# Value products moved behind the next round's scores, and the probabilities divided by ScalarE, in a two-layer trunk kernel

## The chip, the cores and the metric

The kernel runs on one core of a Trainium2 chip. A core has five engines that run in parallel and meet only at semaphores: TensorE (PE, matrix products, with its weight loads shown apart as PEld), VectorE (DVE), ScalarE (ACT), GpSimd (POOL) and SyncE (SP), which here issues the transfers. Each engine takes its own instructions strictly in the order in which the program lists them, so an instruction that waits holds everything behind it on its engine. The metric is the device time of one execution in microseconds (us). The kernel before takes 1017.55 us, the median of 3 runs (1016.76 to 1018.16).

## The reference

Two layers of a decoder trunk on 256 positions of width 1024, in fp32. What matters here is the attention of a layer: 16 heads (A) with a learned sink, and 12 heads (C) in three dilation groups, whose outputs are weighted by their softmax denominators.

```python
for l in range(DEPTH):                                  # DEPTH = 2
    z = rms_norm(x, norm1_g[l]) @ w_in[l] + b_in[l]     # 1024 -> 8448: A, B, C and three gates
    # A and C: banded attention, head size 64
    s = q @ k.T * hd ** -0.5, masked
    m = max(s, -1)                                      # A: also the head's sink
    p = exp(s - m)
    denom = sum(p, -1)                                  # A: + exp(sink - m)
    o = (p / denom) @ v
    # B: spatial gating unit
    x = x + (sum_i sigmoid(gate_i) * (branch_i @ P_i)) @ w_out[l]
    x = x + hier_moe(rms_norm(x, norm2_g[l]), ...)      # 32 experts, top 2 of one group
out = rms_norm(x, norm_f_g)
```

## The kernel before

A layer is a trunk stage (projection, attention, gating, output projection) and an expert stage. The trunk multiplies by weights that stream in through a ring of slots. Every weight slot is a "conv" j: ScalarE rounds it to a high part (`high`, L954), VectorE takes the rest as a low part (`low`, L1161), and PE runs three passes (hi x hi, hi x lo, lo x hi, lines L1509 to L1511) for two halves of the slot and two blocks of 128 positions. A conv is 12 matmuls. Four convs fill one pair of PSUM banks with 512 columns of z, which VectorE then moves out (`z_out`, L1180); for the convs from 44 on this is banks 6 and 7, which every fourth conv starts afresh.

Attention is threaded between the convs 44 to 67, in rounds b = 0 to 11. Rounds 0 to 7 carry two A heads each, rounds 8 to 11 three C heads. In this text the pieces of PE's work have short names:

- Q(b): transposes of q and k for batch b (`qk`, L1613). ScalarE moves them out of PSUM to `qkt` (`qk_out`, L1030). Batches 8 and 10 need three such banks: the first and, for 8, the third go out by ScalarE, the second by VectorE (`swap_out`, L1340 and L1341). Batch 10's third is VectorE's too (L1347). Only two PSUM banks (3 and 4) serve all transposes in turn, so a transpose waits until the one two before it has been moved out (`bank_for`, `turn_taken`, semaphores t_evac and t_swapped). The third transpose of batch 8, called Q3(8) here, stands between the two halves of conv 58.
- S(b): the scores (L1632). VectorE scales, masks and takes the row maximum (`softmax_in`, L1275, L1285), ScalarE takes the exponentials and their row sums (`exps`, L1037), VectorE forms one over the denominator (`softmax_out`, L1303 and L1304, or L1306 to L1309) and multiplies the probabilities with it (L1312).
- T(b): transposes of the divided probabilities (`turn_probs`, L1644), which wait for p_ready. ScalarE moves them out (`pv_out`, L1051).
- P(b): the value products (`product_pair`, L1660, for b below 8; `products`, L1677, for 8 and 9 together after round 9, and for 10 and 11 at the end). ScalarE moves their result out (`o_out`, L1056).

Round b on PE before the change is: conv 44+2b, S(b+1), T(b), conv 45+2b, P(b), Q(b+2), where Q(9) and Q(11) don't exist. ScalarE's list in a round: high 46+2b, pv_out(b), exps(b+1), o_out(b), qk_out(b+2), high 47+2b. VectorE's: softmax_in(b+1), low 46+2b, in odd rounds z_out, in round 6 and 8 swap_out(b+2), softmax_out(b+1), low 47+2b. No scheduler is at work: the order on each engine is the order in which the code calls these helpers.

Of the kernel before, what the change touches and what calls it, by code (L numbers as in the profile page):

```python
# [15 lines left out]
ALU = mybir.AluOpType  # L16
# [8 lines left out]
P = 128  # L25
# [53 lines left out]
def trunk_program(nc, x, positions, norm1_g, w_in, b_in, attn_sinks, sgu_ln_g, sgu_ln_b, w_spatial,  # L79
# [7 lines left out]
    with ExitStack() as whole:  # L87
# [228 lines left out]
        neg_ready = sem("neg_ready")  # L316
# [347 lines left out]
        def trunk_stage(l):  # L664
            with ExitStack():
# [75 lines left out]
                with ExitStack():  # L741
# [191 lines left out]
                    def _(act):  # L933
# [98 lines left out]
                        def exps(b):  # L1032
                            act.wait_ge(neg_ready, 2 * b + 1)
                            i = b % 2
                            for n in range(heads(b)):
                                for tb, lo, hi in ((0, 0, P), (1, P, 3 * P)):
                                    act.activation(probs[:, i, n, lo:hi], probs[:, i, n, lo:hi], ACT.Exp,  # L1037
                                                   bias=neg[:, i, tb, n:n + 1], accum_out=den[:, i, tb, n:n + 1])
                            act.wait_ge(neg_ready, 2 * b + 2)
                            act.activation(ex[:, i, :, 0:heads(b)], ex[:, i, :, 0:heads(b)],  # L1040
                                           ACT.Exp).then_inc(exp_ready, 1)

# [35 lines left out]
                        high_at(45)  # L1078
                        qk_out(1)
                        for b in range(BATCHES):  # L1080
                            if b == 7:
                                halves_at(60)
                            else:
                                high_at(46 + 2 * b)
                            if b == BATCHES - 1:
                                high_at(47 + 2 * b)
                            pv_out(b)
                            if b == 8:
                                qk_out(b + 2, 0, 1)
                            if b == BATCHES - 2:  # L1090
                                high_at(47 + 2 * b)
                            if b + 1 < BATCHES:
                                exps(b + 1)
                            if b < BATCHES - 1:
                                o_out(b)
                            if b + 2 < BATCHES:
                                qk_out(b + 2, 1 if b == 8 else 0)
                            if b < BATCHES - 2:
                                high_at(47 + 2 * b)
                            if b in SPLITS:  # L1100
                                o_high(SPLITS.index(b))
# [37 lines left out]
                    def _(dve):  # L1139
# [125 lines left out]
                        def softmax_in(b, between=None):  # L1265
# [19 lines left out]
                            dve.tensor_scalar(neg[:, i, :, 0:n], m, -1.0, None, ALU.mult).then_inc(neg_ready, 1)  # L1285
                            if b < 8:
                                dve.tensor_tensor(ex[:, i, :, 0:n], sk, m, ALU.subtract).then_inc(neg_ready, 1)

                        def group_max(b):
# [5 lines left out]
                                              ALU.subtract).then_inc(neg_ready, 1)  # L1295

                        def softmax_out(b):
# [4 lines left out]
                            if b < 8:  # L1302
                                link(dve.tensor_tensor(d, d, e, ALU.add))  # L1303
                                link(dve.reciprocal(d, d))  # L1304
                            else:
# [3 lines left out]
                                link(dve.tensor_tensor(d, e, bcast(mxg[:, i, :].unsqueeze(2), [P, TB, n]), ALU.mult))  # L1309
# [169 lines left out]
                    def _(pe):  # L1479
# [202 lines left out]
                        def pv(b, between=None):  # L1682
# [6 lines left out]
                            gates_conv(45 + 2 * b, (lambda: turn_probs(b, 2)) if b >= 8 else None)  # L1689
                            if b < 8:  # L1690
                                product_pair(b)
                            elif b % 2:
                                products(b)
# [16 lines left out]
                        for b in range(BATCHES - 1):  # L1710
# [5 lines left out]
                            else:  # L1716
                                scores(b + 1)
                                pv(b)
# [938 lines left out]
```

## Time and profile before

| what | us |
|---|---|
| median of 3 runs | 1017.55 |
| the profiled execution, its own time | 1017.79 |
| its span on the core | 1015.8 |
| PE busy in the span | 956.4 (94%) |
| DVE busy | 561.1 (55%) |
| ACT busy | 431.3 (42%) |

The profile is of one execution, and its rows are in microseconds from the start of its span. Lines as L1312 are lines of the kernel before. In a timeline row a duration covers the instruction from its start to its end, and neighbours on an engine overlap, so the pace of a row of instructions is read from start to start. In brackets stands how long the engine sat idle before an instruction and what ended that. The rounds of the first layer lie between 125 and 240 us, those of the second between 626 and 741 us, at the same distances.

### The profile page before, as it was taken

To read this page: it belongs to the slowest core of one execution; us is meant where nothing else is said; L and a number is where in the kernel's file an instruction comes from. 1 tells how busy PE (TensorE), PEld (TensorE's weight loads), DVE (VectorE), ACT (ScalarE), POOL (GpSimd) and SP (SyncE) were. 2 spreads that over 40 slices of the span, in tenths; PEclk is the share of its full clock that TensorE was granted. 3 is DMA by queue.
4 is the path that set the end of the run, shared out by engine and by line. 5 is a ranking of instruction groups with operands and counts; after the bars stand their busy time and mean duration, and the time that the engine had idled before them with its cause. 6 is when DMAs were issued, how large, how long until landed. Compare 5 with 4: busy or idle time off the path is not lost.

```text
span 1015.8 us, 15605 instructions
## 1 busy us (share of the span) xinstructions
PE 956.4 (94%) x5898; PEld 667.0 (66%) x5898; DVE 561.1 (55%) x1328; ACT 431.3 (42%) x920; POOL 58.5 (6%) x74
## 2 busy tenths in 40 slices
PE   9999999999999996986999999999999999977887
PEld 7888877778886441532588888777888954444323
DVE  7666787886883332221276668788868634222212
ACT  5434666666444120210353355666764441111122
POOL 1120400000010000000003004000000100000000
PEclk9999999999999998998999999999999999999989
DMA  9975644238999999999997756332599999999996
GB/s 347 352 242 193 193 138 125 84 118 328 359 385 425 404 426 423 426 427 427 418 395 242 240 178 199 125 125 67 175 356 341 407 424 407 426 422 426 426 428 278
DMA packets 99738, 313.03 MB, mean 308 GB/s; under 512 B 13488, under 2 KB 22736, under 8 KB 77648
## 3 DMA queue, kind: packets, MB, share of 16 engines
q1 hardware_dynamic: 99328, 312.04, 80.3%
q8 instruction: 44, 0.72, 0.3%
q14 instruction: 30, 0.25, 0.1%
q10 hardware_dynamic: 336, 0.02, 0.0%
HBM read 310.20 MB, written 1.84 MB: 307 GB/s over the span
## 4 chain that ended last, share of the span: by engine, by line
PE 77%; DMA 13%; SPq 5%; DVE 2%; issue 1%; ACT 1%; DVEq 0%; POOL 0%; POOLq 0%
PE ps L1509 16%; PE ps L1510 15%; PE ps L1511 15%; PE ps L2180 7%; DMA arena<-in_w_expert_up_dram 5%; DMA ring_rest<-in_w_expert_down_dram 5%; SPq L519 5%; PE ps L2154 3%; DMA ring_rest<-in_w_expert_up_dram 3%; PE ps L2257 3%; PE ps L1632 2%; PE ps L1534 2%; PE ps L2269 2%; PE ps L1644 2%; PE ps L2123 2%; PE ps L1660 1%
## 5 line engine op out<-in xcount | busy, mean ns | idle before, releaser
L1161 DVE TENSOR_TENSOR split_w<-arena,split_w 128x512 fp32r<-128x512 f32 (+1 forms) x352 | 233.1, 701 | 100.9 <-ACT split_w L954 97.4
L1509 PE MATMUL ps<-split_w,split_a 128*128 128x512 f32 (+1 forms) x736 | 283.8, 386 | 0.1
L1511 PE MATMUL ps<-split_w,split_a 128*128 128x512 f32 (+1 forms) x736 | 277.0, 376 | 0.0
L1510 PE MATMUL ps<-split_w,split_a 128*128 128x512 f32 (+1 forms) x736 | 276.8, 376 | 0.0
L954 ACT CAST split_w<-arena 128x1024 fp32r<-128x1024 f32 (+1 forms) x171 | 176.0, 1032 | 176.7 <-PE ps L1511 169.9
L1509 PEld LDWEIGHTS ps<-split_w,split_a 128*128 128x128 f32 x736 | 138.5, 188 | 26.9 <-issue 2.2
L1511 PEld LDWEIGHTS ps<-split_w,split_a 128*128 128x128 f32 x736 | 138.4, 188 | 25.9
L1510 PEld LDWEIGHTS ps<-split_w,split_a 128*128 128x128 f32 x736 | 138.7, 188 | 23.2
L2414 DVE SCALAR_TENSOR_TENSOR acts<-ps,wslot,acts 128x256 f32<-128x256 f32 x16 | 7.7, 484 | 167.6 <-ACT acts L2076 145.7
L2180 PE MATMUL ps<-arena,rows 128*32 128x512 f32 x416 | 91.4, 622 | 7.0 <-DMA arena<-in_w_expert_up_dram 6.2
L2180 PE MATMUL ps<-ring_rest,rows 128*32 128x512 f32 x352 | 77.3, 642 | 11.2 <-DMA arena<-in_w_expert_up_dram 11.2
L2154 PEld LDWEIGHTS ps<-arena,work 128*128 128x128 f32 x448 | 54.3, 201 | 28.9 <-issue 24.8
L2154 PE MATMUL ps<-arena,work 128*128 128x128 f32 x448 | 57.2, 288 | 15.7 <-issue 8.9
L2076 ACT ACTIVATE acts<-ps,rslot 128x256 f32<-128x256 f32 x16 | 7.6, 474 | 150.7 <-PE ps L2180 147.4
L2269 PE MATMUL ps<-rows,st 128*128 128x512 f32 x112 | 55.3, 617 | 0.9 <-DVE xs L2395 0.7
L1037 ACT ACTIVATE probs<-probs,neg 128x128 f32<-128x128 f32 x112 | 49.6, 446 | 10.5 <-DVE neg L1285 10.5
L2257 PE MATMUL ps<-arena,acts 128*32 128x512 f32 x264 | 45.2, 621 | 5.2 <-ACT acts L2080 5.2
L1180 DVE SCALAR_TENSOR_TENSOR arena<-ps,rstd,arena 128x512 f32<-128x512 f32 (+2 forms) x68 | 47.2, 729 | 3.9 <-PE ps L1511 3.7
L2180 PEld LDWEIGHTS ps<-ring_rest,rows 128*32 128x32 f32 x352 | 20.0, 117 | 41.6 <-issue 41.6
L2180 PEld LDWEIGHTS ps<-arena,rows 128*32 128x32 f32 x416 | 23.8, 114 | 34.9 <-issue 34.0
L2398 DVE TENSOR_TENSOR xs<-ps,xs 128x512 f32<-128x512 f32 x48 | 33.2, 692 | 18.2 <-PE ps L2269 18.2
L2431 DVE COPY rows<-ps 128x512 f32<-128x512 f32 x14 | 9.7, 692 | 52.2 <-PE ps L2257 52.2
(286 smaller groups left out, 1083.9 us busy)
## 6 DMA issues: line engine op xcount, KB each, us to landing
arena<-in_w_in_dram SPq DMA_DIRECT2D x62, 1024.0 KB, 5.2
arena<-in_w_expert_down_dram SPq DMA_DIRECT2D x34, 1024.0 KB, 21.2
arena<-in_w_expert_up_dram SPq DMA_DIRECT2D x32, 1024.0 KB, 23.5
arena<-in_w_expert_gate_dram SPq DMA_DIRECT2D x32, 1024.0 KB, 24.7
ring_rest<-in_w_expert_down_dram SPq DMA_DIRECT2D x24, 1024.0 KB, 16.9
ring_rest<-in_w_expert_gate_dram SPq DMA_DIRECT2D x22, 1024.0 KB, 23.2
ring_rest<-in_w_expert_up_dram SPq DMA_DIRECT2D x22, 1024.0 KB, 25.3
arena<-in_w_proj_a_dram SPq DMA_DIRECT2D x8, 1024.0 KB, 4.9
```

The lines of the kernel that those rows point to most:

```text
L519: sp.dma_start(slot[:, cols], expert_rows(l, pos)[:, cols]).then_inc(done, 16)
L954: act.copy(whi[:, jj % 2, 0:2 * w], half_slot(jj, w)).then_inc(hi_ready, 1)
L1037: act.activation(probs[:, i, n, lo:hi], probs[:, i, n, lo:hi], ACT.Exp, bias=neg[:, i, tb, n:n + 1], accum_out=den[:, i, tb, n:n + 1])
L1161: dve.tensor_tensor(wlo[:, jj % 2, cols], half_slot(jj, w)[:, cols], whi[:, jj % 2, cols].bitcast(F32), ALU.subtract).then_inc(low_split i ...
L1180: dve.scalar_tensor_tensor(out=z[:, tb, cols], in0=ps[:, bank + tb, 0:w], scalar=rstd[:, tb:tb + 1], in1=z[:, 0, cols], op0=ALU.mult, op1= ...
L1509: pe.matmul(o, hi, rhs_hi, start=first, stop=False)
L1510: pe.matmul(o, hi, rhs_lo, start=False, stop=False)
L1511: return pe.matmul(o, lo, rhs_hi, start=False, stop=last)
L2154: mm = pe.matmul(ps[:, 4 + k // 4, (k % 4) * QUAD:(k % 4 + 1) * QUAD], work[:, tb, k * P:(k + 1) * P], onehot[:, n % 2, tb, :], start=(tb ...
L2180: mm = pe.matmul(ps[e * EC:(e + 1) * EC, n % 2, :].rearrange("p (a f) -> p a f", a=2), xsel[:, k, e * EC:(e + 1) * EC], w, start=(k == 0), ...
L2257: mm = pe.matmul(ps[e * EC:(e + 1) * EC, 2 + nh, :], at_sb[:, kf, e * EC:(e + 1) * EC], w, start=(kf == 0), stop=(kf == 1), skip_group_che ...
L2269: pe.matmul(ps[:, 4 + tb, :], st[:, n % 2, tb * P:(tb + 1) * P], y[:, nh * BANK:(nh + 1) * BANK], start=True, stop=True).then_inc(R.back_r ...
```

## The change

Three things move. P(b-1) goes from behind conv 45+2(b-1) to between S(b+1) and T(b), from round 1 on; with it ScalarE's o_out(b-1) goes in front of pv_out(b). The multiplication by one over the denominator goes from VectorE (two instructions a round over all heads) to ScalarE (`divided`: one instruction per head and block, a copy with the reciprocal as scale of each row), for batches 0 to 10; batch 11 stays on VectorE. And ScalarE's list in a round becomes: high 46+2b, o_out(b-1), pv_out(b), exps(b+1), high 47+2b, divided(b+1), qk_out(b+2). The semaphore neg_ready is renamed row_ready and counts a third event per batch, the reciprocal.

```diff
--- before.py
+++ after.py
@@ -313,7 +313,7 @@
         t_swapped = sem("t_swapped")
         s_ready = sem("s_ready")
         s_free = sem("s_free")
-        neg_ready = sem("neg_ready")
+        row_ready = sem("row_ready")
         exp_ready = sem("exp_ready")
         p_ready = sem("p_ready")
         pv_mm = sem("pv_mm")
@@ -1030,15 +1030,24 @@
                                 act.copy(qkt[:, to, 0:w], ps[:, 3 + t % 2, 0:w]).then_inc(t_evac, 1)
 
                         def exps(b):
-                            act.wait_ge(neg_ready, 2 * b + 1)
+                            act.wait_ge(row_ready, 3 * b + 1)
                             i = b % 2
                             for n in range(heads(b)):
                                 for tb, lo, hi in ((0, 0, P), (1, P, 3 * P)):
                                     act.activation(probs[:, i, n, lo:hi], probs[:, i, n, lo:hi], ACT.Exp,
                                                    bias=neg[:, i, tb, n:n + 1], accum_out=den[:, i, tb, n:n + 1])
-                            act.wait_ge(neg_ready, 2 * b + 2)
+                            act.wait_ge(row_ready, 3 * b + 2)
                             act.activation(ex[:, i, :, 0:heads(b)], ex[:, i, :, 0:heads(b)],
                                            ACT.Exp).then_inc(exp_ready, 1)
+
+                        def divided(b):
+                            act.wait_ge(row_ready, 3 * b + 3)
+                            i = b % 2
+                            for tb, lo, hi in ((0, 0, P), (1, P, 3 * P)):
+                                for n in range(heads(b)):
+                                    last = act.activation(probs[:, i, n, lo:hi], probs[:, i, n, lo:hi], ACT.Copy,
+                                                          scale=den[:, i, tb, n:n + 1])
+                                last.then_inc(p_ready, 1)
 
                         def pv_out(b):
                             for i in range(heads(b)):
@@ -1076,6 +1085,7 @@
                         halves_at(44)
                         exps(0)
                         high_at(45)
+                        divided(0)
                         qk_out(1)
                         for b in range(BATCHES):
                             if b == 7:
@@ -1084,6 +1094,8 @@
                                 high_at(46 + 2 * b)
                             if b == BATCHES - 1:
                                 high_at(47 + 2 * b)
+                            if b >= 1:
+                                o_out(b - 1)
                             pv_out(b)
                             if b == 8:
                                 qk_out(b + 2, 0, 1)
@@ -1091,12 +1103,11 @@
                                 high_at(47 + 2 * b)
                             if b + 1 < BATCHES:
                                 exps(b + 1)
-                            if b < BATCHES - 1:
-                                o_out(b)
+                            if b < BATCHES - 2:
+                                high_at(47 + 2 * b)
+                                divided(b + 1)
                             if b + 2 < BATCHES:
                                 qk_out(b + 2, 1 if b == 8 else 0)
-                            if b < BATCHES - 2:
-                                high_at(47 + 2 * b)
                             if b in SPLITS:
                                 o_high(SPLITS.index(b))
 
@@ -1282,9 +1293,9 @@
                             m = mx[:, i, :, 0:n]
                             if b < 8:
                                 sk = bcast(sinks[:, n * b:n * b + n].unsqueeze(1), [P, TB, n])
-                            dve.tensor_scalar(neg[:, i, :, 0:n], m, -1.0, None, ALU.mult).then_inc(neg_ready, 1)
+                            dve.tensor_scalar(neg[:, i, :, 0:n], m, -1.0, None, ALU.mult).then_inc(row_ready, 1)
                             if b < 8:
-                                dve.tensor_tensor(ex[:, i, :, 0:n], sk, m, ALU.subtract).then_inc(neg_ready, 1)
+                                dve.tensor_tensor(ex[:, i, :, 0:n], sk, m, ALU.subtract).then_inc(row_ready, 1)
 
                         def group_max(b):
 
@@ -1292,7 +1303,7 @@
                             m = mx[:, i, :, 0:n]
                             link(dve.tensor_reduce(mxg[:, i, :], m, AX, ALU.max))
                             dve.tensor_tensor(ex[:, i, :, 0:n], m, bcast(mxg[:, i, :].unsqueeze(2), [P, TB, n]),
-                                              ALU.subtract).then_inc(neg_ready, 1)
+                                              ALU.subtract).then_inc(row_ready, 1)
 
                         def softmax_out(b):
 
@@ -1301,12 +1312,16 @@
                             d, e = den[:, i, :, 0:n], ex[:, i, :, 0:n]
                             if b < 8:
                                 link(dve.tensor_tensor(d, d, e, ALU.add))
-                                link(dve.reciprocal(d, d))
+                                dve.reciprocal(d, d).then_inc(row_ready, 1)
                             else:
                                 link(dve.tensor_tensor(d, d, e, ALU.mult))
                                 link(dve.tensor_reduce(mxg[:, i, :], d, AX, ALU.add))
                                 link(dve.reciprocal(mxg[:, i, :], mxg[:, i, :]))
-                                link(dve.tensor_tensor(d, e, bcast(mxg[:, i, :].unsqueeze(2), [P, TB, n]), ALU.mult))
+                                dve.tensor_tensor(d, e, bcast(mxg[:, i, :].unsqueeze(2), [P, TB, n]),
+                                                  ALU.mult).then_inc(row_ready, 1)
+                            if b < BATCHES - 1:
+                                return
+                            dve.wait_ge(row_ready, 3 * b + 3)
                             for tb, lo, hi in ((0, 0, P), (1, P, 3 * P)):
                                 p = probs[:, i, 0:n, lo:hi]
                                 dve.tensor_tensor(p, p, bcast(den[:, i, tb, 0:n].unsqueeze(2), [P, n, hi - lo]),
@@ -1687,6 +1702,8 @@
                             else:
                                 turn_probs(b, 0, 1)
                             gates_conv(45 + 2 * b, (lambda: turn_probs(b, 2)) if b >= 8 else None)
+
+                        def products_of(b):
                             if b < 8:
                                 product_pair(b)
                             elif b % 2:
@@ -1715,6 +1732,7 @@
                                 pv(b, lambda: scores(1))
                             else:
                                 scores(b + 1)
+                                products_of(b - 1)
                                 pv(b)
                             if b + 2 < BATCHES:
                                 qk(b + 2)
```

The order of instructions shows where things come to stand. First PE in round 6 of a layer, from the end of conv 57 to T(7), before (L1660 is P(6), L1613 Q(8) and Q3(8), L1632 S(8), L1644 T(7)):

```order
L1660 MATMUL ps<-mixed,arena 64x256 [waits o_evac,t_evac]
...
L1613 MATMUL ps<-ident,arena 128x128 [waits t_evac,roped]
...
L1613 MATMUL ps<-ident,arena 128x128 [waits t_evac]
...
L1613 MATMUL ps<-ident,arena 128x128 [waits t_evac,roped]
L1613 MATMUL ps<-ident,arena 128x128 x3
L1509 MATMUL ps<-split_w,split_a 128x512 [waits low_split]
...
L1632 MATMUL ps<-qkt 128x128 [waits s_free,t_evac,t_swapped]
...
L1644 MATMUL ps<-ident,probs 128x128 [waits t_swapped,p_ready]
```

The same stretch after (L1628 is Q(8) and Q3(8), L1647 S(8), L1675 P(6), L1659 T(7)):

```order
L1628 MATMUL ps<-ident,arena 128x128 [waits t_evac,roped]
...
L1628 MATMUL ps<-ident,arena 128x128 [waits t_evac]
...
L1628 MATMUL ps<-ident,arena 128x128 [waits t_evac,roped]
L1628 MATMUL ps<-ident,arena 128x128 x3
L1524 MATMUL ps<-split_w,split_a 128x512 [waits low_split]
...
L1647 MATMUL ps<-qkt 128x128 [waits s_free,t_evac,t_swapped]
...
L1675 MATMUL ps<-mixed,arena 64x256 [waits o_evac,t_evac]
...
L1659 MATMUL ps<-ident,probs 128x128 [waits t_swapped,p_ready]
```

P(6) has left its place ahead of Q(8); the wait of Q3(8) for t_evac, in the middle of conv 58, is as it was.

Then ScalarE in the same round, before (L1040 ends exps(7), L1056 is o_out(6), L1030 qk_out(8) for its first and third bank, L954 high 59, L1060 the high part of an attention output):

```order
L1040 ACTIVATE ex<-ex 128x2x2 [waits neg_ready]
L1056 COPY arena<-ps 128x2x128 [waits pv_mm]
L1030 COPY qkt<-ps 128x512 [waits t_ready] x2
L954 CAST split_w<-arena 128x1024 [waits conv_used,ring_in1]
L1060 CAST split_a<-arena 128x512 [waits o_evac]
```

and after (L954 is high 59, L1048 divided(7), L1030 qk_out(8), L1069 the former L1060):

```order
L1040 ACTIVATE ex<-ex 128x2x2 [waits row_ready]
L954 CAST split_w<-arena 128x1024 [waits conv_used,ring_in1]
L1048 ACTIVATE probs<-probs,den 128x128 [waits row_ready]
L1048 ACTIVATE probs<-probs,den 128x128
L1048 ACTIVATE probs<-probs,den 128x256 x2
L1030 COPY qkt<-ps 128x512 [waits t_ready] x2
L1069 CAST split_a<-arena 128x512 [waits o_evac]
```

qk_out(8) now stands behind high 59 and behind divided(7), which waits for VectorE's reciprocal.

## Rows read from the trace of the kernel before

**Rows 1.** The page, first part: busy us, share, instructions of PE.

```profile
PE 956.4 (94%) x5898; PEld 667.0 (66%) x5898; DVE 561.1 (55%) x1328; ACT 431.3 (42%) x920; POOL 58.5 (6%) x74
```

**Rows 2.** Waits from 195 to 245 us: us in total, times, longest.

```profile
PEld ps L1644 <- DVE probs L1312: 0.9, 3, 0.4
```

**Rows 3.** Timeline of PE, rounds 6 and 7: start us, us, line, operation, tiles.

```profile
190.65 0.87 PE L1660 MATMUL ps<-mixed,arena 128*64 128x256 f32 x8
191.45 1.09 PE L1613 MATMUL ps<-ident,arena 128*128 128x128 f32 x8
...
193.77 0.60 PE L1613 MATMUL ps<-ident,arena 128*128 128x128 f32 x4
```

**Rows 4.** Timeline of DVE in round 6: swap_out(8), then softmax_out(7).

```profile
192.58 0.69 DVE L1340 COPY qkt<-ps 64x512 f32<-64x512 f32 x1 [2.44 <-PE ps L1613]
...
194.20 0.18 DVE L1304 RECIPROCAL den<-den 128x4 f32<-128x4 f32 x1
194.41 1.03 DVE L1312 TENSOR_TENSOR probs<-probs,den 128x256 f32<-128x256 f32 x2
```

**Rows 5.** Timeline of ACT in round 6: the first bank of qk_out(8).

```profile
192.14 0.59 ACT L1030 COPY qkt<-ps 128x512 f32<-128x512 f32 x1 [0.18 <-PE ps L1613]
```

**Rows 6.** Timeline of ACT, one head's exponentials: 128 columns, then 256.

```profile
201.27 0.39 ACT L1037 ACTIVATE probs<-probs,neg 128x128 f32<-128x128 f32 x1
201.56 0.19 ACT L1037 ACTIVATION_READ_ACCUMULATOR probs<-probs,neg 128x1 f32 x1
201.66 0.50 ACT L1037 ACTIVATE probs<-probs,neg 128x256 f32<-128x256 f32 x1
...
202.06 0.19 ACT L1037 ACTIVATION_READ_ACCUMULATOR probs<-probs,neg 128x1 f32 x1
```

**Rows 7.** Timeline of ACT, copies from PSUM with a scale per row.

```profile
302.31 0.83 ACT L606 ACTIVATE rows<-ps,gains 128x256 f32<-128x256 f32 x2
...
410.65 1.14 ACT L2048 ACTIVATE rows<-ps,gain 128x128 f32<-128x128 f32 x4 [17.61 <-PE ps L2154]
```

**Rows 8.** Timeline, round 0: high 45, qk_out(1), and PE's S(1).

```profile
133.44 1.04 ACT L954 CAST split_w<-arena 128x1024 fp32r<-128x1024 f32 x1
135.26 0.37 ACT L1030 COPY qkt<-ps 128x256 f32<-128x256 f32 x1 [0.79 <-PE ps L1613]
...
135.69 0.93 PE L1632 MATMUL ps<-qkt 64*128 64x128 f32 x8
```

**Rows 9.** Timeline, round 8 into 9: high 63 and 64, division, T(9).

```profile
213.78 1.56 ACT L954 CAST split_w<-arena 128x1024 fp32r<-128x1024 f32 x2
...
214.70 1.43 DVE L1312 TENSOR_TENSOR probs<-probs,den 128x384 f32<-128x384 f32 x2
...
216.19 0.66 PE L1644 MATMUL ps<-ident,probs 128*128 128x128 f32 x4 [0.15 <-DVE probs L1312]
```

**Rows 10.** Timeline, rounds 7 and 9: second z_out, PE's conv 60 and 64.

```profile
201.18 0.74 DVE L1180 SCALAR_TENSOR_TENSOR arena<-ps,rstd,arena 128x512 f32<-128x512 f32 x1
...
202.40 0.40 PE L1509 MATMUL ps<-split_w,split_a 128*128 128x512 f32 x1
...
220.44 0.74 DVE L1180 SCALAR_TENSOR_TENSOR arena<-ps,rstd,arena 128x512 f32<-128x512 f32 x1
...
222.65 0.28 PE L1509 MATMUL ps<-split_w,split_a 128*128 128x256 f32 x1
```

**Rows 11.** PE after a long wait in the expert stage.

```profile
467.72 1.08 PE L2180 MATMUL ps<-ring_rest,rows 128*32 128x512 f32 x3 [5.26 <-DMA arena<-in_w_expert_up_dram]
```

**Rows 12.** Windows: busy us of PE, PEld, DVE, ACT, POOL; PEclk, DMA share, GB/s.

```profile
464.80:465.00 0.20, 0.00 (x0) 0.00 (x0) 0.00 (x0) 0.00 (x0) 0.00 (x0) 0.87 1.07 451
471.60:471.80 0.20, 0.20 (x4) 0.00 (x0) 0.00 (x0) 0.00 (x0) 0.00 (x0) 0.56 1.06 451
```

**Rows 13.** Windows, DMA share around the end of the rounds.

```profile
220.00:230.00 10.00, 10.00 (x88) 8.78 (x88) 7.97 (x33) 7.36 (x26) 0.00 (x0) 1.00 0.66 196
...
240.00:250.00 10.00, 10.00 (x66) 7.99 (x65) 4.31 (x7) 5.48 (x7) 0.00 (x0) 1.00 1.01 360
```

## The prediction

> **What bounds the kernel now.** I read first the page's busy times: PE works 956.4 of 1015.8 us [rows 1]. Then the waits in the window of the attention rounds: of PE's waits for the work that this change touches, only three for VectorE's division are left in rounds 8 to 11, 0.9 us in all [rows 2]. So the rounds are bound by PE's own order, ScalarE and VectorE have idle time in them, and taking work off VectorE can give back little. What decides is whether the new order makes PE wait. For that I went through the timelines of PE, VectorE and ScalarE round by round and laid the new order over the old times.
>
> **The division, part by part.** VectorE loses two instructions a round for batches 0 to 10: 1.03 us of pace for two heads [rows 4], 1.43 us for three [rows 9]. None of that stood ahead of PE except in the waits named. ScalarE gains four instructions a round (two of 128 columns, two of 256), six for three heads. The trace before has none of exactly this form. The nearest are the exponentials: same source, same target, same columns, one operand per row. From their start to the read that follows passes 0.29 us at 128 and 0.40 at 256 columns [rows 6]; I take 0.30 and 0.40, so 1.4 us for two heads and 2.1 us for three. The lower end is a copy with a scale per row from PSUM: four of 128 columns in 1.14 us end, less 0.37 for the last, 0.26 each, and two of 256 in 0.83 us, 0.36 each [rows 7]; 1.24 and 1.86 us. The upper end is the exponential with its read, 0.39 and 0.49 [rows 6]; 1.76 and 2.64 us. It can't be below nothing: the work is added to ScalarE's list.
>
> The Trainium skill ("ScalarE: Activation LUTs", "What ACT_TABLE_LOAD costs") says that an operand per row adds about 93 ns to an instruction, whatever the function. By that the division would cost as the exponential without its read, which is my value rather than the cheaper rows 7; an estimate from its formula gives 1.39 us for two heads. The sum doesn't need it.
>
> **Place one, round 6: the third bank of batch 8.** This carries the sum. Q3(8) stands inside conv 58 and waits until ScalarE has moved out the first bank of Q(8). Before, ScalarE did this right behind o_out(6), at 192.14 to 192.73 [rows 5], and Q3(8) began at 193.77 without a wait [rows 3]. Now it stands behind high 59 and divided(7). divided(7) waits for the reciprocal of batch 7, and VectorE makes that only after swap_out(8), which itself waits for the second bank of Q(8). Step by step:
> - P(6) leaves its place, so Q(8) begins where P(6) did, at 190.65 and not 191.45 [rows 3]: 0.80 earlier. Q3(8) would then be due at 193.77 - 0.80 = 192.97.
> - VectorE's swap_out(8) began 1.13 us after Q(8) (192.58 against 191.45), so now at 191.78. From there to the end of the reciprocal, where the old division could start, it is 194.41 - 192.58 = 1.83 us [rows 4]: 193.61.
> - high 59 is over by then: it needs conv 57 (done about 190.7) and takes 1.05 us. So divided(7) runs from 193.63 to 195.03, and the copy of 0.59 us [rows 5] ends at 195.62.
> - PE goes on at about 195.67. That is 195.67 - 192.97 = 2.70 us of PE standing still. Lower end 2.5, upper end 3.1.
> Behind PE's wait stand the second half of conv 58, S(8), P(6), T(7) and everything after. Nothing gives it back.
>
> **Place two, round 0.** S(1) needs qk_out(1), which now stands behind divided(0), and T(0)'s first head needs the division. high 45 begins at 133.44 and lets the next begin 0.95 later, at 134.39; the reciprocal is ready at about 134.0. Divided until 135.79, copy of 0.37 us until 136.16, S(1) at 136.20 where it was 135.69 [rows 8]: 0.51 us. Lower end 0.35, upper end 0.9.
>
> **Place three, round 9.** T(9) already waits for the division: the old one ended at 214.70 + 1.43 = 216.13, and T went on at 216.19 [rows 9]. Now ScalarE first does high 63 (213.78 to 214.73), then six instructions: the last begins 1.70 later and takes 0.50, so it ends at 216.93. The exponentials hang on Q(10) as before, so both times shift alike: 0.80 us more. Lower end 0.5, upper end 1.3.
>
> **Place four, after convs 59 and 63.** In rounds 7 and 9 no Q follows, so when P goes, conv 60 (64) stands right behind conv 59 (63), on the banks that VectorE is still moving out. P covered that. VectorE's second z_out ended at 201.18 + 0.74 = 201.92, and conv 60's second block began at 202.40 [rows 10]. Without P (0.80 at its new place) it can't begin before about 201.94, so the stretch costs 201.94 + 0.80 - 202.40 = 0.34 us. For conv 64: 220.44 + 0.74 + 0.05 = 221.23, plus 2.10 for the double product, less 222.65 [rows 10]: 0.68 us. Both are 1.0 us together; the lower end is -0.4 (no wait, and two changes from one kind of matmul to another saved at 0.2 each), the upper end 1.3.
>
> **What else moves costs nothing.** In rounds 1 to 5 divided(b+1) and qk_out(b+2) end 1 to 2 us before T(b+1) needs them, because high 47+2b was not needed until then. T(8) and T(10) are due 0.3 us or more after their division: T(10) is the closest, and at the upper end of the price it is late by 0.4 us. o_out(b-1) stands ahead of pv_out(b) and waits for P(b-1), which PE does just before T(b); pv_out is then about half a microsecond later and its only reader is a round away. P costs the same 0.80 at its new place. T(11) is still divided by VectorE. No transfer moves but with PE.
>
> **The sum.** Per layer 2.70 + 0.51 + 0.80 + 1.02 = 5.0 us; the second layer has the same order and the same distances, so 10.1 us. Lower ends: 2.5 + 0.35 + 0.5 - 0.4 = 3.0, twice 5.9. Upper ends: 3.1 + 0.9 + 1.3 + 1.3 + 0.4 = 7.0, twice 14. The profiled execution took 1017.79 us, span 1015.8 and 2.0 around it; it is 0.24 above the median. Against the median: 1017.55 + 10.1 = 1027.6, and I say 1028.
>
> **Rivals.**
> - The clock falls in the new pause (20%, of slower). PE stands still about 2.5 us at place one. In the expert stage PE waited 5.26 us until 467.72 [rows 11], and its granted clock fell from 2.4 to 1.2 GHz at about 464.9, 2.4 us into the wait; it rose again at about 471.7, 4 us after work began [rows 12]. If it falls in the new pause, some 4 us run at half speed and about 2 us are lost, per layer: 1030 for one, 1032 for both. The Trainium skill has this rule ("TensorE: Matmul & The Clock Gate", "HAM oscillation — how this bites in real kernels"): a gap between matmuls can drop the gate to the cold clock, and the work after it pays. The trace agrees for the wait of 5.26 us; no row here shows what a pause of 2.7 us inside the rounds does.
> - A part of the places is hidden (20%): the division is as cheap as rows 7, and place four has no wait. Then 1017.55 + 5.9 = 1023.5.
> - Absorbed by transfers (4%, no change): the expert stages are full of transfers, and a late trunk might find them waiting less. For it: the DMA share is 1.01 from 240 us on. Against it: it is 0.66 between 220 and 230 [rows 13], since the transfers wait for slots that PE and VectorE free, so they start as much later. 1017.6.
> - The gain side (5%, faster): VectorE is the one that decides in rounds 8 to 11. If VectorE's freed 1.03 to 1.43 us a round let the reciprocal, the low parts and z_out come earlier than I lay them, and Q3(8) were not held, then PE's 0.9 us of waits per layer [rows 2] would go and two changes of kind at 0.2 us each: 1017.55 - 2.6 = 1014.9. It decides if qk_out(8) starts before 192.4 in round 6; for that divided(7) would have to be over before its own reciprocal, so the order speaks against it.
> - The division by ScalarE costs as if it were much slower than any row here (part of the upper tail, 3%): above 1033.
>
> **How the numbers follow.** The forecast 1028 holds 48%, the clock 20%, the hidden part 20%, slower in the tail 3%, no change 4%, gain 5%. The range from 1022.5 to 1032.5 takes in the hidden part and the clock and leaves out under 2 in 10. A difference of 0.2% (2.0 us) is about what a measurement of this kernel can tell from none. Faster 0.05, within 0.04, slower 0.91.
>
> **What would show it.** In the changed profile: PE idle inside conv 58 before Q3(8) for about 2.7 us, released by ScalarE's copy to qkt, once in each layer; four or six copies with a scale by ScalarE behind high 47+2b, at 0.3 to 0.4 us; S(1) about half a microsecond later; T(9) waiting for ScalarE about 0.8 us longer; short waits of conv 60 and 64 for VectorE's z_out. The expert stages as long as before. It would be wrong if Q3(8) begins within a few tenths of the end of conv 58's first half, or if VectorE's reciprocal of batch 7 comes well before 193.6.

## The result and the profile after

The changed kernel took 1032.8 us (median of 4 runs, 1032.31 to 1033.9), the kernel before 1017.5 beside it: ratio 1.0152, 95% interval 1.014 to 1.0163. It is slower by 15.3 us where 10.5 were forecast, just above the range. The profiled execution took 1033.02 us with a span of 1030.9; before it was 1017.79 and 1015.8, so the two traces differ by 15.1 in the span.

The first part of the page after, as in [rows 1]: busy us, share of the span, instructions.

```profile
PE 961.5 (93%) x5898; PEld 670.8 (65%) x5898; DVE 536.9 (52%) x1284; ACT 464.0 (45%) x1020; POOL 58.6 (6%) x74
```

VectorE works 24.2 us less and ScalarE 32.7 us more, as the change says. PE has the same 5898 instructions and is 5.1 us longer busy, and the rest of the 15.1 is idle time. The division by its two shapes (busy us, mean ns of one, then idle us ahead of it and what ended that):

```profile
L1048 ACT ACTIVATE probs<-probs,den 128x256 f32<-128x256 f32 x50 | 22.0, 494 | 0.0
L1048 ACT ACTIVATE probs<-probs,den 128x128 f32<-128x128 f32 x50 | 17.0, 393 | 8.5 <-DVE den L1315 6.6 <-DVE den L1320 1.9
```

Now the waits of PE and of its weight loads in 125 to 252 us, the first layer's rounds: us in total, times, longest.

```profile
PE ps L1628 <- ACT qkt L1030: 2.6, 1, 2.6
PE ps L1659 <- ACT probs L1048: 1.2, 2, 0.8
PE ps L1647 <- ACT qkt L1030: 0.8, 3, 0.3
PE ps L1524 <- DVE arena L1191: 0.7, 3, 0.3
...
PEld ps L1647 <- ACT qkt L1030: 3.5, 7, 0.7
```

In the kernel before, PE itself has one wait in such a list, of 0.2 us. The first line is Q3(8), place one. The second is T(0) and T(9), places two and three. The fourth holds convs 60 and 64, place four. The third was not forecast: the scores wait for ScalarE's copy to qkt.

**The pause.** PE around it:

```profile
194.19 0.39 PE L1526 MATMUL ps<-split_w,split_a 128*128 128x512 f32 x1
197.18 0.63 PE L1628 MATMUL ps<-ident,arena 128*128 128x128 f32 x4 [2.60 <-ACT qkt L1030]
...
199.66 2.63 PE L1647 MATMUL ps<-qkt 64*128 64x128 f32 x12
```

VectorE and then ScalarE in the same stretch:

```profile
193.25 0.69 DVE L1355 COPY qkt<-ps 64x512 f32<-64x512 f32 x1 [2.20 <-PE ps L1628]
...
194.86 0.18 DVE L1315 RECIPROCAL den<-den 128x4 f32<-128x4 f32 x1
```

```profile
192.43 1.05 ACT L954 CAST split_w<-arena 128x1024 fp32r<-128x1024 f32 x1 [0.23 <-PE ps L1526]
195.08 1.49 ACT L1048 ACTIVATE probs<-probs,den 128x128 f32<-128x128 f32 x4 [1.60 <-DVE den L1315]
196.47 0.56 ACT L1030 COPY qkt<-ps 128x512 f32<-128x512 f32 x1
```

The chain is the one forecast, link by link: Q(8)'s second bank, swap_out(8) (193.25), reciprocal (194.86), four divisions (195.08), copy (196.47), Q3(8) (197.18). Without the wait Q3(8) would follow 0.23 us behind the conv matmul of 194.19, so 197.18 - 194.42 = 2.76 us are lost; [rows 3] has it without a wait.

**What came behind it.** S(8) takes 2.63 us; the same 12 instructions take 1.57 as S(10). The windows say why (busy us of PE, PEld, DVE, ACT, POOL; then the granted clock, DMA share, GB/s):

```profile
195.00:196.00 1.00, 0.00 (x0) 0.00 (x0) 1.00 (x3) 0.92 (x3) 0.00 (x0) 1.00 0.00 0
...
197.80:198.20 0.40, 0.40 (x4) 0.32 (x3) 0.00 (x0) 0.35 (x1) 0.00 (x0) 1.00 0.62 174
198.20:198.60 0.40, 0.40 (x3) 0.32 (x2) 0.00 (x0) 0.40 (x2) 0.00 (x0) 0.81 0.97 323
198.60:199.60 1.00, 1.00 (x3) 0.33 (x1) 0.62 (x1) 0.35 (x1) 0.00 (x0) 0.50 0.75 265
...
201.80:202.20 0.40, 0.40 (x2) 0.06 (x1) 0.00 (x0) 0.00 (x0) 0.00 (x0) 0.92 0.00 0
```

The granted clock stays at 1.00 (2.4 GHz) through the whole pause and for another 1.3 us of work, falls to 0.50 (1.2 GHz) between 198.4 and 198.5 and is back at about 201.9. The second layer has the same: a pause of 2.60 us before 705.74, and 0.50 from about 707.0 to 710.4. PE waits for nothing there, so no list of waits shows this loss.

**The scores that wait.** S(3) on PE, and what ScalarE did before it:

```profile
152.50 0.93 PE L1647 MATMUL ps<-qkt 64*128 64x128 f32 x8 [0.28 <-ACT qkt L1030]
```

```profile
150.70 1.50 ACT L1048 ACTIVATE probs<-probs,den 128x128 f32<-128x128 f32 x4 [0.57 <-DVE den L1315]
152.10 0.34 ACT L1030 COPY qkt<-ps 128x256 f32<-128x256 f32 x1
```

The copy qk_out(3) is S(3)'s input. It ends at 152.44 and S(3) begins at 152.50. Before, it ran from 149.66 to 150.03, with S(3) at 152.31: 2.3 us to spare. Now high 49 (from 149.08), the wait for the reciprocal and divided(2) stand ahead of it, and it ends 2.4 us later.

**Places two, three and four.** T(0), T(9) and conv 64 on PE:

```profile
135.80 0.44 PE L1659 MATMUL ps<-ident,probs 128*128 128x128 f32 x2 [0.47 <-ACT probs L1048]
136.17 0.93 PE L1647 MATMUL ps<-qkt 64*128 64x128 f32 x8
...
220.36 1.57 PE L1647 MATMUL ps<-qkt 64*128 64x128 f32 x12
...
223.22 0.66 PE L1659 MATMUL ps<-ident,probs 128*128 128x128 f32 x4 [0.76 <-ACT probs L1048]
...
227.25 0.36 PE L1524 MATMUL ps<-split_w,split_a 128*128 128x256 f32 x1 [0.24 <-DVE arena L1191]
```

S(1) was at 135.69 [rows 8] with S(0) at 128.41. Now it is at 136.17 with S(0) at 128.29, which is 0.60 more. It stands directly behind the two transposes of T(0) that waited 0.47 us for the division; its own input, the copy qk_out(1), ended at 136.01. T(9)'s marked row comes 2.86 us behind S(10); before it came 216.19 - 214.09 = 2.10 behind it [rows 9].

**By milestones.** The start of each S(b) on PE after S(0), in us, worked out from PE's timelines of the first layer. B is the first transpose behind the rounds. The second layer agrees within 0.11.

| kernel | S(1) | S(3) | S(7) | S(8) | S(9) | S(10) | S(11) | B |
|---|---|---|---|---|---|---|---|---|
| before | 7.28 | 23.90 | 57.81 | 67.28 | 76.16 | 85.68 | 95.41 | 114.16 |
| after | 7.88 | 24.21 | 58.74 | 71.37 | 81.75 | 92.07 | 101.05 | 121.89 |
| products only | 7.28 | 23.07 | 56.94 | 66.28 | 75.62 | 85.93 | 94.35 | 115.21 |
| products where no Q follows stay | 7.28 | 23.06 | 56.93 | 66.27 | 75.96 | 85.47 | 95.20 | 113.94 |
| first bank ahead | 7.89 | 24.20 | 58.74 | 68.86 | 78.09 | 88.40 | 97.39 | 118.23 |
| qk_out first | 7.89 | 23.72 | 57.62 | 67.75 | 77.04 | 87.35 | 96.32 | 117.17 |
| division only | 7.89 | 24.52 | 58.42 | 68.68 | 77.48 | 87.00 | 97.30 | 116.14 |
| pause filled, 20 | 7.89 | 24.21 | 58.74 | 72.53 | 81.82 | 92.13 | 101.11 | 121.95 |
| pause filled, 10 | 7.88 | 24.19 | 58.75 | 70.86 | 80.20 | 90.52 | 99.48 | 120.33 |
| reciprocal first | 7.88 | 24.19 | 58.74 | 69.14 | 78.49 | 88.79 | 97.76 | 118.60 |
| all mended | 7.28 | 23.06 | 56.92 | 66.26 | 75.94 | 85.46 | 95.19 | 114.02 |

Where P(b-1) stands behind S(b+1) and not ahead of it, an S comes some 0.8 us earlier by its place alone, so kernels are compared in column B, or with one that has P at the same place. After against before is 7.73 us in B, twice that is 15.5, and 15.1 is the difference in the span: all of the loss lies in the rounds, and about 0.3 us is won outside them.

### The profile page after: what moved, and what is told of

The parts are those of the page before. It is cut to its first block, busy times and chain, and to the rows that moved or that the text cites. A ratio compares the mean times of both kernels' runs of the same rounds, so it can differ in the third digit from the quotient of the medians.

```text
span 1030.9 us, 15661 instructions
## 1 busy us (share of the span) xinstructions
PE 961.5 (93%) x5898; PEld 670.8 (65%) x5898; DVE 536.9 (52%) x1284; ACT 464.0 (45%) x1020; POOL 58.6 (6%) x74
## 4 chain that ended last, share of the span: by engine, by line
PE 69%; DMA 16%; SPq 5%; ACT 5%; DVE 4%; issue 1%; POOL 0%; DVEq 0%; POOLq 0%; ACTq 0%
PE ps L1524 14%; PE ps L1526 14%; PE ps L1525 14%; PE ps L2198 6%; DMA arena<-in_w_expert_up_dram 5%; DMA ring_rest<-in_w_expert_up_dram 5%; SPq L519 5%; DMA ring_rest<-in_w_expert_down_dram 5%; PE ps L1647 2%; PE ps L2172 2%; PE ps L1549 2%; PE ps L2275 2%; ACT probs L1048 2%; PE ps L1659 2%; PE ps L2141 1%; PE ps L2287 1%
## 5 line engine op out<-in xcount | busy, mean ns | idle before, releaser
L954 ACT CAST split_w<-arena 128x1024 fp32r<-128x1024 f32 (+1 forms) x171 | 175.7, 1029 | 164.7 <-PE ps L1526 157.9
L2198 PE MATMUL ps<-ring_rest,rows 128*32 128x512 f32 x352 | 79.4, 639 | 10.3 <-DMA arena<-in_w_expert_up_dram 10.3
L2172 PEld LDWEIGHTS ps<-arena,work 128*128 128x128 f32 x448 | 54.5, 202 | 23.6 <-issue 15.1
L1191 DVE SCALAR_TENSOR_TENSOR arena<-ps,rstd,arena 128x512 f32<-128x512 f32 (+2 forms) x68 | 47.2, 729 | 15.7 <-PE ps L1526 15.5
L1048 ACT ACTIVATE probs<-probs,den 128x128 f32<-128x128 f32 (+1 forms) x100 | 37.0, 443 | 8.5 <-DVE den L1315 6.6
```

What stands on the lines that cost most here:

```text
L954: act.copy(whi[:, jj % 2, 0:2 * w], half_slot(jj, w)).then_inc(hi_ready, 1)
L1048: last = act.activation(probs[:, i, n, lo:hi], probs[:, i, n, lo:hi], ACT.Copy, scale=den[:, i, tb, n:n + 1])
L2172: mm = pe.matmul(ps[:, 4 + k // 4, (k % 4) * QUAD:(k % 4 + 1) * QUAD], work[:, tb, k * P:(k + 1) * P], onehot[:, n % 2, tb, :], start=(tb ...
L2198: mm = pe.matmul(ps[e * EC:(e + 1) * EC, n % 2, :].rearrange("p (a f) -> p a f", a=2), xsel[:, k, e * EC:(e + 1) * EC], w, start=(k == 0), ...
```

## The experiments

All times are medians beside runs of the kernel before on the same chip (1017.32 for "qk_out first", "first bank ahead", "division only" and "pause filled, 20"; 1017.61 for the two runs with the products alone; 1017.14 for the rest). The diffs show the lines that matter, and what they leave out is said beside them.

**qk_out first.** The changed kernel with the copies of qk_out(b+2) ahead of high 47+2b and the division.

```diff
+if b < 8:
+    qk_out(b + 2, 0, 1 if b == 6 else 3)
 if b < BATCHES - 2:
     high_at(47 + 2 * b)
     divided(b + 1)
-if b + 2 < BATCHES:
-    qk_out(b + 2, 1 if b == 8 else 0)
+if b == 6 or 8 <= b < BATCHES - 2:
+    qk_out(b + 2, 1)
```

> Theory (order on ScalarE): what costs is that qk_out(b+2) stands behind the division, once before the third transpose of batch 8 and in rounds 1, 3 and 5 before the next scores. Here qk_out(b+2) goes ahead of high 47+2b and of the division (for batch 8 only its first bank). Per layer the pause of 2.75 us goes, the slow clock behind it (1.6 us) with it, and three waits of S of about 0.65 us; round 0 stays. 1032.8 - 2 x 6.3 = 1020.2 us. The order of theory's later waits (T(9), conv 60 and 64) stays. Rival (load on ScalarE): the 1.4 to 2.1 us of division a round press on ScalarE wherever they stand; then the waits reappear before T(b) or before the convs' low parts, and the time stays above 1027 us.

**First bank ahead.** Only place one is mended: of the copies, the first bank of batch 8 alone goes ahead.

```diff
+if b == 6:
+    qk_out(b + 2, 0, 1)
 if b < BATCHES - 2:
     high_at(47 + 2 * b)
     divided(b + 1)
 if b + 2 < BATCHES:
-    qk_out(b + 2, 1 if b == 8 else 0)
+    qk_out(b + 2, 1 if b in (6, 8) else 0)
```

> Only in round 6 the first bank of qk_out(8) goes ahead of high 59 and of divided(7); all else is as in the changed kernel. Theory: the pause before the third transpose of batch 8 and the slow clock behind it go, 2 x (2.75 + 1.6) = 8.7 us: 1024.1 us; the waits of S in rounds 1, 3 and 5 stay (2 x 2.0 us). Rival (the pause only hides others: VectorE's swap or the low part of conv 59 are as late): less than half of it, above 1028.5 us.

Measured: qk_out first 1023.91 us (ratio 1.0062, 1.0047 to 1.0078), first bank ahead 1025.87 (1.0083, 1.0068 to 1.0099). The pause and the slow clock are gone in both. In column B they are 1.06 us apart per layer: that is what the scores' waits of rounds 1 to 6 cost, since these copies are all that differs. Both came out slower than expected, the first by 3.7 us and the second by 1.8. About 1.6 of either is a wait that the pause had covered. Most of the rest of the first is the scores' waits: the expectation had taken off 1.95 a layer for them, because I had thought that the moved products win back about 1.0 a layer in the other rounds; they win 0.2 ("products where no Q follows stay"). The covered wait, in the trace of qk_out first, S(8):

```profile
193.44 0.60 PE L1630 MATMUL ps<-ident,arena 128*128 128x128 f32 x4
...
196.14 1.55 PE L1649 MATMUL ps<-qkt 64*128 64x128 f32 x12 [0.72 <-issue]
```

The copy that it needs, on ScalarE:

```profile
194.08 1.50 ACT L1048 ACTIVATE probs<-probs,den 128x128 f32<-128x128 f32 x4 [0.74 <-DVE den L1317]
195.48 0.56 ACT L1030 COPY qkt<-ps 128x512 f32<-128x512 f32 x1
```

The row of S(8) names no releaser, but the copy ends at 196.04, 0.10 us ahead of it. Q3(8) is in time now, and the copy of its bank stands behind divided(7), which costs 0.79 us per layer (S(7) to S(8) against "products only": 10.13 and 9.34).

**Products only.** The kernel before with P(b) and o_out(b) moved as in the change, and VectorE dividing. The diff shows PE's part; on ScalarE o_out(b-1) goes ahead of pv_out(b).

```diff
 scores(b + 1)
+products_of(b - 1)
 pv(b)
```

> The kernel before with P(b-1) moved between S(b+1) and T(b) and o_out(b-1) ahead of pv_out(b), but VectorE divides and qk_out(b+2) stands ahead of high 47+2b as before. Theory: rounds 1 to 6 each get 0.17 us shorter (P joins a group of small matmuls), conv 60 and 64 wait for z_out and cost 1.0 us together: per layer about 0, 1017.5 us, within 1 us. Rival (my first count, in which moving P saves nothing in rounds 1 to 6): 1019.5 us. Rival (P was cover for more than z_out): above 1021 us.

Measured: 1019.95 us (ratio 1.0022, 1.0013 to 1.0031; 11 runs), the rival's side. Column B is 1.05 us above before, which is place four (1.02 forecast) less a small gain that the next run shows apart. That the scores S(2) to S(8) come earlier than before is nearly all P's place.

**Products where no Q follows stay.** The same, but P(7) and the double product of batches 8 and 9 stay behind convs 59 and 63. The diff shows PE's part; o_out of these stays too.

```diff
-products_of(b - 1)
+if b - 1 not in (7, 9):
+    products_of(b - 1)
```

> As e4, but P(7) and the double product of 8 and 9 stay behind conv 59 and 63, where no Q follows. Theory: the 0.17 us a round of rounds 1 to 6 stay, the waits of conv 60 and 64 don't arise: 1017.5 - 2 x 1.0 = 1015.5 us, faster than before by 0.2%. Rival (the 0.17 us are a shift that is given back later): 1017.5 us.

Measured: 1017.2 us (ratio 0.9996, 0.9987 to 1.0005; 11 runs), where 1015.5 was expected: the gain of 0.17 us a round isn't there. Place four is gone. Column B is 1.27 us below "products only", which is what place four costs by itself, and 0.22 below before, of which 0.20 is there by S(9). Twice 0.22 is less than the times can tell from none: where a Q follows, P's move is all but neutral.

**Division only.** ScalarE divides, the products stay, and the copies are ahead of the division as in "qk_out first". The diff is against the changed kernel and shows PE's part; ScalarE's o_out(b) goes back behind exps(b+1).

```diff
 scores(b + 1)
-products_of(b - 1)
 pv(b)
+products_of(b)
 if b + 2 < BATCHES:
     qk(b + 2)
```

> The division by ScalarE alone: P(b) stays behind conv 45+2b as in the kernel before, o_out(b) and qk_out(b+2) stand ahead of high 47+2b, and divided(b+1) behind it (for batch 8 the second copy of qk_out behind the division). Theory: the instructions themselves are hidden, except in round 0 (0.6 us) and before T(9) (0.75 us): 1017.5 + 2 x 1.35 = 1020.2 us. Rival (load on ScalarE): every round loses some tenths, above 1024 us. If the freed VectorE gave something back: below 1017 us.

Measured: 1021.39 us (ratio 1.0036, 1.0022 to 1.005), 1.2 above the expectation, which didn't have the third bank. Column B is 1.98 above before: 0.61 in S(1), 0.79 in S(8) (the third bank again), 0.57 in T(9). The division without any product moved costs about 4 us. In S(1) it is the division itself and not the copy, which stands ahead of it here.

**Pause filled, 20 and 10.** The changed kernel with matmuls of the identity, which nobody reads, between the halves of conv 58, ahead of Q3(8). They keep PE busy and change nothing else (the diff leaves out the call of `third`, which replaces the one of qk).

```diff
+def third():
+    if b == 7:
+        pe.wait_ge(s_free, 8)
+        for _ in range(20):
+            pe.matmul(ps[:, 0, 0:P], ident[:], ident[:], start=True, stop=True)
+    qk(b + 1, 2, 3)
```

> The changed kernel with 20 idle matmuls (128x128, results not used) on PE in the pause before the third transpose of batch 8, some 2.2 us of the 2.75. Theory: the granted clock stays at 2.4 GHz in both layers, S(8) takes 1.6 us and not 2.6, and 2 x 1.6 = 3.2 us go: 1029.6 us, with the pause itself unchanged. Rival (the scores after the pause are slow for another reason, or such matmuls don't hold the clock): S(8) still takes 2.6 us, 1032.8 us or, if they delay the third transpose, more.

Measured: 1032.34 us (ratio 1.0143, 1.0127 to 1.0159), 2.7 above the expectation. The filling was too long: the trace shows 40 instructions for the 20 calls, in 4.63 us, so Q3(8) began at 199.11 though ScalarE's copy had ended at 197.26. The clock stayed at 2.4 GHz and S(8) took 1.57 us, but the time saved there was spent on the filling. As a price for the clock the run is inconclusive, hence the next with half as many.

> The changed kernel, with 10 matmuls that compute nothing wanted between the release of the bank and Q3(8), where the run before this one had 20. 20 took 4.63 us, so 10 take about 2.3 us and end about 0.3 us before ScalarE's copy releases Q3(8) at 197.2: the pause is filled but not lengthened. Theory (the clock fell because PE stood still, and cost 1.6 us per layer): granted clock 1.00 through the round, S(8) 1.57 us, S(9) of layer 0 at S(0) + 80.2 instead of 81.75, and 1032.8 - 3.2 = 1029.6 us in all. Rival (the pause alone is the cost; the slow stretch after it is inside other waits): the clock stays, but S(9) comes no more than 0.3 us earlier, 1032.5 us.

Measured: 1028.88 us (ratio 1.0118, 1.0103 to 1.0133). The filling and what follows it on PE:

```profile
194.39 2.39 PE L1732 MATMUL ps<-ident 128*128 128x128 f32 x20
197.15 0.63 PE L1628 MATMUL ps<-ident,arena 128*128 128x128 f32 x4 [0.36 <-ACT qkt L1030]
...
199.10 1.57 PE L1647 MATMUL ps<-qkt 64*128 64x128 f32 x12
```

Its window in the place where the clock had been at half:

```profile
199.00:201.00 2.00, 2.00 (x17) 1.44 (x18) 1.62 (x5) 1.14 (x2) 0.00 (x0) 1.00 0.21 71
```

Q3(8) begins at the same time as in the changed kernel, but from there to S(9) it is 1.55 us shorter (80.20 against 81.75, as expected), and 1.56 in B. The whole kernel is 3.9 us faster than the changed one (3.6 with each set against the kernel before beside it), of which 3.1 lie in the rounds. So the fall follows from PE standing still, and costs 1.55 us per layer on top of the pause.

**Reciprocal first.** The changed kernel with VectorE's softmax_out(7) ahead of swap_out(8) (left out: `third_out` of round 8, which stays).

```diff
+if b == 6:
+    softmax_out(b + 1)
 if b in (6, 8):
     swap_out(b + 2)
...
-softmax_out(b + 1)
+if b != 6:
+    softmax_out(b + 1)
```

> The changed kernel, with one thing moved: VectorE makes the reciprocal of batch 7 ahead of moving out the second bank of Q(8), not behind it. Theory (the pause is the chain Q(8) second bank, swap_out, reciprocal, divided(7), copy): the reciprocal is ready at about 192.9 instead of 195.04, divided(7) starts right behind high 59 at 193.5, the copy ends at about 195.6, and the pause before Q3(8) is about 1.1 us instead of 2.75; no fall of the clock behind it. Per layer 1.6 us of pause and 1.6 us of clock come back: 1032.8 - 6.4 = 1026.4 us. Rival (the clock falls after a pause of 1.1 us too): 1029.6 us. Rival (the swap, now later, holds S(8) instead): over 1028 us with a wait of S(8) for VectorE.

Measured: 1026.51 us (ratio 1.0091, 1.0075 to 1.0106). PE and ScalarE:

```profile
195.04 0.63 PE L1631 MATMUL ps<-ident,arena 128*128 128x128 f32 x4 [0.90 <-ACT qkt L1030]
...
196.98 1.57 PE L1650 MATMUL ps<-qkt 64*128 64x128 f32 x12
```

```profile
192.93 1.49 ACT L1048 ACTIVATE probs<-probs,den 128x128 f32<-128x128 f32 x4
194.33 0.56 ACT L1030 COPY qkt<-ps 128x512 f32<-128x512 f32 x1
```

The divisions follow high 59 directly, the pause is 0.90 us, and the clock doesn't fall. Two instructions moved on an engine with idle time bring back 6.3 of the 15.3 us, so the swap ahead of the reciprocal was a link of the chain.

**All mended.** The changed kernel with the copies ahead as in "qk_out first", batches 0, 7, 9 and 11 divided by VectorE, and P(7) and the product of 8 and 9 back in their old places. The diff shows the first lines of the division alone.

```diff
 def divided(b):
+    if b in (0, 7, 9, 11):
+        return
```

> The change with every place mended for which a cost has been found: qk_out(b+2) ahead of high 47+2b and the division, batches 0, 7, 9 and 11 divided by VectorE as before, P(7) and P(9) behind convs 59 and 63 as before; all else as in the changed kernel (ScalarE divides eight batches, P(b) behind S(b+2) in the other rounds). Theory (the costs found are all there are): none of the waits of the changed kernel is left, and the time is that of before, 1017.2 us (1016.5 to 1018.0), S(11) of layer 0 at S(0) + 95.3. Rival (a cost of the change was overlooked, such as ScalarE's longer list in rounds 1 to 6): 1019 us or more. Rival on the other side (VectorE's freed microsecond of eight rounds is worth something once nothing else waits): under 1016 us.

Measured: 1018.24 us (ratio 1.001, 1.0001 to 1.0019; 11 runs), 0.2 above the end of the expected range and just clear of the kernel before. In the rounds it is as expected: B is 0.14 below before, and PE itself has no wait in them but the one of 0.2 us that the kernel before has too. The 1.1 us in the median is not in the rounds. In the profiled execution the part of the span behind B of the second layer is 1.1 us longer than before; in the other profiled executions this part is from 1.0 us shorter to 0.2 longer than before. Whether the 1.1 us belongs to the kernel or to the executions stays open. In any case no version beats the kernel before by more than the times can tell: ScalarE can divide eight batches without a wait in the rounds, and nothing is gained by it.

## Why the prediction was short

The terms per layer, in us:

| term | forecast | measured | from |
|---|---|---|---|
| place one, Q3(8) | 2.70 | 2.78 | S(8): pause filled, 10, against products only (4.58), less 1.80 already there in S(7) |
| place two, round 0 | 0.51 | 0.60 | S(1) |
| place three, T(9) | 0.80 | 0.56 | S(10) to S(11), after against products only |
| place four, convs 60 and 64 | 1.02 | 1.05 | B of products only (1.27, less 0.22 that P's move wins elsewhere) |
| scores waiting for qk_out | 0 | 1.20 | S(7) less S(1), after against products only |
| clock behind the pause | 0 (a rival) | 1.55 | B of pause filled, 10 |
| sum | 5.03 | 7.74 | B: 7.73 |

- **Place one** was right in its chain and within 0.1 in its size. The division cost what the exponentials' rows gave: four in 1.49 us, which is 0.30 + 0.30 + 0.40 and a last one of 0.49.
- **Place two** was right within 0.1 in size, and wrong in its last link. The forecast took S(1) from the end of the copy behind divided(0). With the copy ahead of the division S(1) comes no earlier (7.89 in "qk_out first"): what holds it is T(0), which stands ahead of S(1) and waits for the division.
- **Place four** was right in its kind, and its size with some luck: by itself it is 1.27 and not 1.02, and P's move wins back 0.22 that the forecast didn't have.
- **Place three** was 0.24 too high. T(9)'s last four transposes do begin 0.76 us later behind S(10). But the old division also held conv 63, since its low part stands behind the division on VectorE. In "products only", on VectorE and on PE:

```profile
214.40 1.43 DVE L1316 TENSOR_TENSOR probs<-probs,den 128x384 f32<-128x384 f32 x2
215.74 1.29 DVE L1165 TENSOR_TENSOR split_w<-arena,split_w 128x512 fp32r<-128x512 f32 x2
```

```profile
215.88 0.66 PE L1648 MATMUL ps<-ident,probs 128*128 128x128 f32 x4 [0.15 <-DVE probs L1316]
216.48 0.50 PE L1513 MATMUL ps<-split_w,split_a 128*128 128x512 f32 x1
```

The first half of the low part takes 0.68 us where one stands alone, so it is done at about 216.4, and the conv begins at 216.48, 0.60 us behind the marked row. Now it begins 0.41 behind it (223.22 to 223.63), because the low part is over by then. This 0.19 us is the one place where VectorE's freed time pays. I had counted the wait ahead of the transposes only.
- **The step that failed** is "What else moves costs nothing": "In rounds 1 to 5 divided(b+1) and qk_out(b+2) end 1 to 2 us before T(b+1) needs them, because high 47+2b was not needed until then." T(b+1) reads the division, but it doesn't read qk_out(b+2): that is read by S(b+2), which stands directly behind conv 46+2b and ahead of T(b+1). The copy has the earliest deadline of the three and was put last. Measured against S instead of T, the slack before was 2.3 us in round 1. What stands ahead of the copy now, high 49, the wait of 0.57 us for the reciprocal and the division of 1.4, takes from 149.08 to 152.10, and the copy ends 2.4 us later than before. It costs 0.18 to 0.36 us in S(2), S(3), S(5) and S(7), 1.2 per layer; "qk_out first" against "first bank ahead" shows 1.06 of it taken back by the copies' place alone.
- **The clock** was named as a rival at 20%, with "about 2 us" a layer. It took place in both layers, for 1.55 each, where the sum of the forecast put nothing. I gave it too small a chance because the nearest rows [rows 11, 12] had a pause of twice the length. Those rows show the fall 2.4 us into the wait, though, and the forecast pause was 2.7.
- Alone, either of the last two would have left the time in the range: 1028 + 2.4 is 1030.4, 1028 + 3.1 is 1031.1. Together they are 5.5, and the measured 1032.8 is 4.8 above the forecast.
- **The gain side and the absorption** did not happen. VectorE's 24 us came off an engine that PE hardly waited for: the 0.9 us of [rows 2] are waits of its weight loads, and PE itself waited 0.2. Of the rounds' 15.5 us the span shows 15.1, so next to nothing was taken back elsewhere.

## What to carry to other kernels

When a step is put ahead of others on an in-order engine, list every instruction behind it, and for each the reader with the earliest deadline; a pair that "ends in time" for one reader may be late for another. A pause on TensorE is priced with the slow stretch that can follow it, and this stretch stands in no list of waits: compare the length of the same matmuls behind the pause. And when a wait is mended, look for the one that it covered, as the third bank of batch 8 here.

## What the hardware showed

- The clock fell after work had resumed: PE stood still for 2.60 us at a granted 1.00, worked 1.3 us at 1.00, and had 0.50 for the next 3.4 us, in both layers. Pauses of 0.72 us ("qk_out first", before S(8)) and 0.90 us ("reciprocal first", before Q3(8)) were followed by no fall. The Trainium skill ("TensorE: Matmul & The Clock Gate", "HAM oscillation — how this bites in real kernels") has a gap between matmuls as the cause; the runs with the gap filled bear this out: the granted clock stays at 1.00 in both, and "pause filled, 10" gives back 1.55 us per layer.
- A plain f32 matmul with 128 columns runs as two instructions of 0.12 us each (40 for 20 calls, 4.63 us), where a transpose of the same shape runs as one: 8 of Q(8) for 8 blocks, in 1.03 us.
